# One modulation chunk per k tile, the first of them multiplied ahead of x and its sums, with idle products before it

## The chip, the cores and the metric

The kernel runs on one core of one Trainium2 chip. The metric is device time in microseconds (us) of one execution, as the median of several runs; less is better. The engines are TensorE (PE, its weight loads PEld), VectorE (DVE), ScalarE (ACT), GpSimd (POOL) and SyncE (SP), which issues most of the DMAs.

## What is computed

One step of a diffusion backbone with one trunk layer, for 128 context tokens and 512 latent tokens, 640 tokens in all, each 1024 wide. Cut to what the change touches:

```python
mod_ctx = jax.nn.silu(c_ctx)[None, :] @ w_mod[l] + b_mod[l]      # context tokens
mod_lat = jax.nn.silu(c) @ w_mod[l] + b_mod[l]                   # latent tokens
shift1, scale1, gate1, shift2, scale2, gate2 = [m[:, None, :] for m in jnp.split(mod, 6, axis=-1)]
h = _rmsnorm(x, g_norm1) * (1 + scale1) + shift1
proj = h @ w_in + b_in
q_raw, k_raw, v_raw, o_raw, gates, u_pool, g_a, g_b = jnp.split(proj, split_at, axis=-1)
```

Behind this come the mLSTM, the pooling branch, the merge, a mixture of 16 experts and a final norm. They are computed as before. So all 640 tokens need the sum of the squares of their 1024 elements (`_rmsnorm`), and each of the 1024 channels needs its shift1 and scale1 for two conditioning vectors, before any column of `w_in` can be multiplied.

## The kernel before

x lies with channels on partitions, in eight k tiles of 128 channels by 640 tokens (`xT[:, k, :]`). Every engine's program is written out by hand and runs strictly in that order; semaphores join them. The start of the kernel, which is the part that changes, is this:

- **SP** (lines 436 to 459) issues on one queue: all constants (`small`, 1440 columns), the four DMAs of x (two k tiles each), the gate weights `wgr`, and then the weight stream `wst`, 1 MB chunks in a fixed order, through four buffers (`raw`). Chunk 0 (`AT_U0`) is the first half of the pool columns of `w_in`; chunks 1 to 8 (`AT_M1`, `N_MOD1`) are the columns of `w_mod` for shift1 and scale1; chunk 9 (`AT_U1`) is the second half of the pool columns. A chunk is issued when its buffer is free (`raw_free`).
- **ACT** (698 to 722) applies tanh to the conditioning vectors, squares the eight k tiles into `hn`, rounds `wgr` and chunk 0 into their high parts, forms the reciprocal norm `rstd` with Ln and Exp (`inv_rms`), and then, for each of four pairs of k tiles, copies one row of modulation products out of PSUM (`mrow1`), forms `hn = hn * gain + shift` (L717, in two parts, context and latent), and copies it rounded to `hhi` (L721).
- **DVE** (1145 to 1186) finishes silu (`csil`), adds the eight squares up in `hn[:, 0]` (L1158), forms the low parts of the weights, multiplies x by `rstd` (L1165), forms `mod` and `gain` of each pair (L1179, L1182) and the low part `hlo = hn - hhi` (L1169).
- **PE** (2038 to 2056): `square_sums` multiplies the summed squares by a matrix of ones (two f32 products of 320 columns); `mod_pair(i)` takes two chunks (8 f32 products of 512 columns, four side by side in the array) and gives shift1 and scale1 of two k tiles, as rows; `mod_turned(i)` turns these rows to columns with four small products; `pool_outer(k)` adds k tile k to the gate and pool outputs, 18 products of 320 columns, each operand in a high and a low part (`three`). All of it stands in this order, with the `pool_outer` of early k tiles between the modulation products of later ones:

```python
            square_sums(hn, s_sum1, s_norm)
            pe.wait_ge(s_csil, 3)
            mod_pair(0)
            mod_turned(0)
            mod_pair(1)
            pe.wait_ge(s_gw, 2)
            pe.wait_ge(s_norm, 2)
            chunk_split(0)
            pool_outer(0)
            mod_turned(1)
            pool_outer(1)
            mod_pair(2)
```

After the eighth `pool_outer` the second half of the pool columns follows, and then the rest of the kernel, a PE stream with few gaps.

An f32 product leaves two records in the trace, so eight records of line 1964 are four products, or one chunk. Products whose operands are rounded (`hhi`, `hlo`, `whi` and the like) leave one. `keep_busy(n)` (1941) issues n f32 products of 256 columns on constants whose result nobody reads; the kernel uses it around the router.

Of the kernel before, what the change touches and what calls it, by code (L numbers as in the profile page):

```python
# [54 lines left out]
N_MOD1 = 8  # L55
N_U, N_GE, N_Q, N_K, N_MOD2, N_V, N_O, N_GL, N_B, N_A, N_OUT = 2, 6, 4, 4, 16, 4, 4, 2, 2, 4, 4
# [13 lines left out]
C_ID, C_ONE, C_FWD, C_BWD, C_STRICT, C_IOTA, C_NEGF, C_NEGB = (P * i for i in range(8))  # L70
C_MF = 8 * P
# [14 lines left out]
S_COL = 1088  # L86
# [39 lines left out]

def split_no(c):
    if c > AT_V:
        return N_U + N_K + 1 + c - AT_V
    if c >= AT_K:  # L130
        return N_U + 1 + (c - AT_K + 2) // 5
    return 1 if c == AT_U0 else 2
# [28 lines left out]
def raw_slot(c):  # L161
    return (c - AT_O) % 2 if AT_O <= c < AT_A else c % NRAW
# [22 lines left out]
def layer_kernel(nc, x_d, small_d, wst_d, wg_d, wpool_d, st_d, rcnt_d,  # L185
                 wexp_d, xt_d, gf_d, bv_d, y_d, so_d, mo_d):
    ctx = ExitStack()
    with ctx:
# [45 lines left out]
        rstd = at("rstd", 172.5, [P, T])  # L234
        QK = at("QK", 112, [P, 2 * H, T])
# [4 lines left out]
        mrow1 = at("mrow1", TMP + 5, [P, 2, 512])  # L240
# [127 lines left out]
        def f32(t):  # L368
# [15 lines left out]
        s_csil, s_sq, s_norm, s_hn, s_hhi, s_hlo = (sem(n) for n in (  # L384
            "s_csil", "s_sq", "s_norm", "s_hn", "s_hhi", "s_hlo"))
        d_wg, s_gain = sem("d_wg"), sem("s_gain")
# [50 lines left out]
        def _(sp):  # L437
            sp.dma_start(small[:, :], small_d).then_inc(d_const, 16)
            for k in range(0, KT, 2):
                sp.dma_start(xT[:, k:k + 2, :], x_d[:, k:k + 2, :]).then_inc(d_tile[k // 2], 16)  # L440
            sp.dma_start(wgr[:, :, :], wg_d).then_inc(d_wg, 16)
# [8 lines left out]
            for c in range(N_DENSE):  # L450
# [4 lines left out]
                sp.dma_start(raw[s][:, :], wst_d[c, :, :]).then_inc(raw_full[s], 16)  # L455
                if c == AT_V + 1:
# [57 lines left out]
        def _(gp):  # L514
# [58 lines left out]
            gp.wait_ge(s_modT, 6)  # L573
# [107 lines left out]
        def _(act):  # L681
# [21 lines left out]
            act.wait_ge(d_wg, 16)  # L703
            act.activation(wgh[:, :, :], wgr[:, :, :], ACT.Copy).then_inc(s_gw, 1)
            act.preload_act_table_set(LN_EXP)
            split_hi(0, QH[0])
            act.wait_ge(s_norm, 1)
            inv_rms(halves(rstd[:, :]), ps[:, 0:2, 0:HALF], D, s_norm)
            for i in range(4):
                chunk_used(act, AT_M1 + 2 * i + 1)  # L710
                if i >= 2:
                    act.wait_ge(s_modT, i - 1)
                act.activation(mrow1[:, i % 2, :], ps[:, 4, :], ACT.Copy).then_inc(s_mrow, 1)
                act.wait_ge(s_gain, i + 1)
                for k in (2 * i, 2 * i + 1):
                    for c, a, b in ((0, 0, TC), (1, TC, T)):
                        act.activation(hn[:, k, a:b], hn[:, k, a:b], ACT.Identity,  # L717
                                       bias=mod[:, k, c:c + 1], scale=gain[:, k, c:c + 1])\
                           .then_inc(s_hn, 1)
                    act.wait_ge(s_hn, 2 * k + 2)  # L720
                    act.activation(hhi[:, k, :], hn[:, k, :], ACT.Copy).then_inc(s_hhi, 1)  # L721
# [78 lines left out]
            def mod_row2(i):  # L800
                chunk_used(act, m2_chunk(KT * i + KT - 1))
                if i:
                    act.wait_ge(s_modT, i + 4)
# [197 lines left out]
            act.preload_act_table_set(LN_EXP)  # L1001
            act.activation(strict[:, :], cst[:, C_STRICT:C_STRICT + P], ACT.Copy)
# [128 lines left out]
        def _(dve):  # L1131
# [21 lines left out]
            st.on(dve.tensor_scalar(half_gn[:, :], col[:, G_N:G_N + KT], 0.5, None, ALU.mult))  # L1153
            for k in range(1, KT):
# [7 lines left out]
            split_lo(0, QH[0], QL[0])  # L1162

            def normalise(k):
                st.on(dve.tensor_tensor(hn[:, k, :], xT[:, k, :], rstd[:, :], ALU.mult))  # L1165

            def input_lo(k):
                dve.wait_ge(s_hhi, k + 1)
                dve.tensor_tensor(hlo[:, k, :], hn[:, k, :], f32(hhi[:, k, :]), ALU.subtract)\  # L1169
                   .then_inc(s_hlo, 1)  # L1170

            dve.wait_ge(s_norm, 2)
            for k in range(4):
                normalise(k)
            for i in range(4):
                dve.wait_ge(s_modT, i + 1)
                both = mod[:, 0:16, :].rearrange("p (s k) c -> p s k c", s=2)[:, :, 2 * i:2 * i + 2, :]
                bias = col[:, B_MOD:B_MOD + 16].rearrange("p (s k) -> p s k", s=2)
                st.do(dve.tensor_tensor(both, ps[:, 5, 0:8].rearrange(  # L1179
                    "p (s k c) -> p s k c", s=2, c=2), by(bias[:, :, 2 * i:2 * i + 2].unsqueeze(3),  # L1180
                                                          [P, 2, 2, 2]), ALU.add))
                dve.scalar_tensor_tensor(  # L1182
                    gain[:, 2 * i:2 * i + 2, :], mod[:, 8 + 2 * i:10 + 2 * i, :], 1.0,
                    by(col[:, G_1 + 2 * i:G_1 + 2 * i + 2].unsqueeze(2), [P, 2, 2]), ALU.add, ALU.mult)\
                   .then_inc(s_gain, 1)
                if i < 2:
                    normalise(4 + 2 * i)
                    normalise(5 + 2 * i)
                for k in (2 * i, 2 * i + 1):
                    input_lo(k)  # L1190
# [116 lines left out]
            def mod_add(i):  # L1307
                dve.wait_ge(s_modT, i + 5)
# [174 lines left out]
            dve.wait_ge(s_gt, 3)  # L1483
            mask_maxima(0)
# [432 lines left out]
        def _(pe):  # L1917
# [41 lines left out]
            def mod_half(c, kh, bank):  # L1959

                slot = raw_slot(c)
                pe.wait_ge(raw_full[slot], (raw_use(c) + 1) * 16)
                for kk in range(4):
                    last = nc.tensor.matmul(  # L1964
                        ps[32 * kk:32 * kk + 32, bank, :], csil[:, 4 * kh + kk, :],
                        raw[slot][:, kk * 512:(kk + 1) * 512], start=kh == 0, stop=kh == 1,
                        tile_position=(0, 32 * kk))
                last.then_inc(raw_free[slot], 1)
# [11 lines left out]
            def mod_columns(rows, out):  # L1980
                for b in range(4):
                    last = mm(out[:, 2 * b:2 * b + 2], rows[:, b * P:(b + 1) * P],
# [11 lines left out]
            def pool_outer(k):  # L1994
                pe.wait_ge(s_hlo, k + 1)
                last = three([(ps[0:GP, 6 + a, 0:HALF], cut_half(a)) for a in range(2)],
                             wgh[:, k, :], wgl[:, k, :], hhi[:, k, :], hlo[:, k, :],
                             k == 0, k == KT - 1)
                if k == KT - 1:
                    last.then_inc(s_gate, 1)  # L2000
                for b in range(2):
                    o = (b * KT + k) * P
                    last = three([(ps[:, 2 * b + a, 0:HALF], cut_half(a)) for a in range(2)],
                                 QH[0][:, o:o + P], QL[0][:, o:o + P], hhi[:, k, :], hlo[:, k, :],
                                 k == 0, k == KT - 1)
# [657 lines left out]
```

## Time and profile before

| | |
|---|---|
| median of 3 runs | 968.03 us (966.66 to 969.24) |
| profiled execution, its own time | 965.73 us |
| its span | 963.9 us |
| PE busy | 929.9 us, 96% of the span |
| DVE, ACT, POOL busy | 698.6, 495.3, 134.8 us |
| moved by DMA | 229.51 MB, mean 238 GB/s |

The span is the time from the first to the last instruction in the trace; 1.8 us of the execution lie around it. PE is busy in nearly all of the span except its first fortieth, where its digit in the page's slices is 3.

### The profile page before, as it was taken

To read this page: it belongs to the slowest core of one execution; us is meant where nothing else is said; L and a number is where in the kernel's file an instruction comes from. 1 tells how busy PE (TensorE), PEld (TensorE's weight loads), DVE (VectorE), ACT (ScalarE), POOL (GpSimd) and SP (SyncE) were. 2 spreads that over 40 slices of the span, in tenths; PEclk is the share of its full clock that TensorE was granted. 3 is DMA by queue.
4 is the path that set the end of the run, shared out by engine and by line. 5 is a ranking of instruction groups with operands and counts; after the bars stand their busy time and mean duration, and the time that the engine had idled before them with its cause. 6 is when DMAs were issued, how large, how long until landed. Compare 5 with 4: busy or idle time off the path is not lost.

```text
span 963.9 us, 14007 instructions
## 1 busy us (share of the span) xinstructions
PE 929.9 (96%) x5518; PEld 819.8 (85%) x5518; DVE 698.6 (72%) x895; ACT 495.3 (51%) x656; POOL 134.8 (14%) x141
## 2 busy tenths in 40 slices
PE   3999999999999999999999999989999999999986
PEld 1799999988788999999999988868888888888862
DVE  5398777649223478889454546369999999999998
ACT  5565442231222356666411232246788787887863
POOL 0000000089920111000000000020111111111100
PEclk9999999999999999999999999979999999999998
DMA  9812443287762342434382155159999999999964
GB/s 380 335 45 90 152 134 101 83 333 274 278 258 113 91 135 87 122 121 161 136 338 88 44 188 227 45 197 394 421 421 404 422 416 411 420 414 419 392 274 163
DMA packets 39201, 229.51 MB, mean 238 GB/s; under 512 B 4288, under 2 KB 4480, under 8 KB 18528
## 3 DMA queue, kind: packets, MB, share of 16 engines
q1 hardware_dynamic: 26496, 180.25, 47.6%
q0 software_dynamic: 10048, 41.70, 12.2%
q10 hardware_dynamic: 2592, 6.66, 1.8%
q8 instruction: 44, 0.72, 0.3%
q14 instruction: 21, 0.17, 0.0%
HBM read 205.94 MB, written 22.66 MB: 237 GB/s over the span
## 4 chain that ended last, share of the span: by engine, by line
PE 92%; DMA 4%; DVE 3%; ACT 1%; issue 0%; SPq 0%; DVEq 0%; POOLq 0%; ACTq 0%
PE ps L1919 86%; PE ps L2444 2%; PE ps L1975 2%; DMA h2scr<-ht 1%; DMA xT<-in_x 1%; PE ps L2472 1%; DMA raw<-in_wst 1%; PE ps L1964 1%; DMA xg<-h2scr,slot_rows 0%; PE ps L2286 0%; PE ps L2187 0%; DVE rowA L1874 0%; DVE xr L1877 0%; DVE xr L1881 0%; PE ps L2363 0%
## 5 line engine op out<-in xcount | busy, mean ns | idle before, releaser
L690 ACT ACTIVATE whi<-raw 128x2048 fp32r<-128x2048 f32 x19 | 36.3, 1912 | 96.6 <-PE ps L1919 63.7
L1919 PE MATMUL ps<-hhi,whi 128*128 128x320 f32 x352 | 81.2, 312 | 0.0
L1919 PE MATMUL ps<-hlo,whi 128*128 128x320 f32 x352 | 80.2, 309 | 0.0
L1919 PE MATMUL ps<-hhi,wlo 128*128 128x320 f32 x352 | 80.2, 309 | 0.0
L1730 DVE TENSOR_TENSOR olo<-raw,ohi 128x2048 fp32r<-128x2048 f32 x32 | 72.3, 2286 | 3.9 <-ACT ohi L1042 3.9
L1138 DVE TENSOR_TENSOR wlo<-raw,whi 128x2048 fp32r<-128x2048 f32 x19 | 43.9, 2311 | 42.0 <-ACT whi L690 42.0
L1730 DVE TENSOR_TENSOR wlo<-raw,whi 128x2048 fp32r<-128x2048 f32 x31 | 70.3, 2288 | 5.3 <-ACT whi L1042 4.7
L1042 ACT ACTIVATE whi<-raw 128x2048 fp32r<-128x2048 f32 x32 | 61.3, 1918 | 18.4 <-PE ps L1919 18.4
L1042 ACT ACTIVATE ohi<-raw 128x2048 fp32r<-128x2048 f32 x32 | 61.3, 1917 | 18.0 <-PE ps L1919 18.0
L1919 PEld LDWEIGHTS ps<-hhi,whi 128*128 128x128 f32 x352 | 58.6, 188 | 6.2 <-issue 5.0
L1919 PEld LDWEIGHTS ps<-hhi,wlo 128*128 128x128 f32 x352 | 58.9, 188 | 0.0
L1919 PEld LDWEIGHTS ps<-hlo,whi 128*128 128x128 f32 x352 | 58.8, 188 | 0.0
L1919 PE MATMUL ps<-whi,xgh 128*128 128x512 f32 x128 | 50.9, 398 | 0.0
L1919 PE MATMUL ps<-ohi,xgh 128*128 128x512 f32 x128 | 50.8, 397 | 0.0
L1919 PE MATMUL ps<-ohi,xgl 128*128 128x512 f32 x128 | 50.0, 391 | 0.0
L1919 PE MATMUL ps<-whi,xgl 128*128 128x512 f32 x128 | 50.0, 390 | 0.0
L1919 PE MATMUL ps<-wlo,xgh 128*128 128x512 f32 x128 | 49.8, 389 | 0.0
L1919 PE MATMUL ps<-olo,xgh 128*128 128x512 f32 x128 | 49.8, 389 | 0.0
L1919 PE MATMUL ps<-Tlo,ghi 128*128 128x320 f32 x160 | 49.4, 309 | 0.0
L1919 PE MATMUL ps<-Thi,ghi 128*128 128x320 f32 x160 | 49.4, 309 | 0.0
L1919 PE MATMUL ps<-hhi,owh 128*128 128x320 f32 x160 | 49.3, 324 | 0.1
L1919 PE MATMUL ps<-hhi,owl 128*128 128x320 f32 x160 | 46.9, 309 | 0.0
(424 smaller groups left out, 2551.3 us busy)
## 6 DMA issues: line engine op xcount, KB each, us to landing
raw<-in_wexp SPq DMA_DIRECT2D x64, 1024.0 KB, 9.0
raw<-in_wst SPq DMA_DIRECT2D x60, 1024.0 KB, 6.1
eraw<-in_wexp SPq DMA_DIRECT2D x32, 1024.0 KB, 8.8
nm<-negscr POOLq DMA_DIRECT2D x8, 640.0 KB, 7.1
wib<-wiscr POOLq DMA_DIRECT2D x8, 512.0 KB, 6.3
thscr<-gout ACTq DMA_DIRECT2D x12, 320.0 KB, 5.2
TH<-thscr POOLq DMA_DIRECT2D x3, 1280.0 KB, 7.4
xT<-in_x SPq DMA_DIRECT2D x4, 640.0 KB, 7.1
```

What stands on the lines that cost most here:

```text
L690: act.activation(dst[:, :], raw[raw_slot(c)][:, :], ACT.Copy).then_inc(hi_ready, 1)
L1042: act.activation(ehi[i % ESPL][:, :], eraw[s][:, :], ACT.Copy).then_inc(e_hi, 1)
L1138: dve.tensor_tensor(lo[:, :], raw[s][:, :], f32(hi[:, :]), ALU.subtract)\
L1730: dve.tensor_tensor(elo[i % ESPL][:, :], eraw[s][:, :], f32(ehi[i % ESPL][:, :]), ALU.subtract).then_inc(e_free[s], 1)
L1919: return nc.tensor.matmul(out, lhsT, rhs, start=start, stop=stop)
L1964: last = nc.tensor.matmul(ps[32 * kk:32 * kk + 32, bank, :], csil[:, 4 * kh + kk, :], raw[slot][:, kk * 512:(kk + 1) * 512], start=kh == 0 ...
L1975: last = nc.tensor.matmul(ps[32 * g:32 * g + 32, 6, :], csil[:, k, :], raw[slot][:, g * 512:(g + 1) * 512], start=k == 0, stop=k == KT - 1 ...
L2444: last = nc.tensor.transpose(ps[:, 6 + k // 4, (k % 4) * P:(k % 4 + 1) * P], xg[b][:, k * P:(k + 1) * P], ident)
L2472: last = nc.tensor.transpose(ps[:, 2 * (p % 2), f * P:(f + 1) * P], act_[:, f * P:(f + 1) * P], ident)
```

## The change

It has four parts, all in the start of the kernel.

1. **The modulation goes by k tile.** The eight chunks of `w_mod` are laid out anew on the host, so that one chunk holds shift1 and scale1 of one k tile (256 columns, all 1024 inputs) instead of half the inputs of two k tiles. `mod_product(k)` has 8 products of 256 columns and `mod_turned(k)` two small ones. `outer_hi(k)` and `outer_lo(k)` are the 18 products of `pool_outer(k)`, in two parts.
2. **The first chunk comes ahead.** SP issues a part of the constants (360 columns), then modulation chunk 0, and only then x. PE multiplies it ahead of `square_sums`, and DVE's `mod_row(0)` and `gains(0)` stand ahead of the sums of squares.
3. **Idle products.** Before `mod_product(0)` PE runs 28 f32 products of 186 columns on constants, whose result nobody reads.
4. **Parted loads and other edges.** Chunk 0 of the weights has a buffer of its own (`u0r`) and comes in two DMAs, rounded in three parts; the rest of the constants comes after the last modulation chunk (`d_late`). ACT writes `hhi` straight from x in one step, and DVE forms the unrounded `hn` itself (`modulated`). The constants' columns are in another order.

```diff
-            sp.dma_start(small[:, :], small_d).then_inc(d_const, 16)
-            for k in range(0, KT, 2):
-                sp.dma_start(xT[:, k:k + 2, :], x_d[:, k:k + 2, :]).then_inc(d_tile[k // 2], 16)
-            sp.dma_start(wgr[:, :, :], wg_d).then_inc(d_wg, 16)
+            sp.dma_start(small[:, C_ONE:S_WR], small_d[:, C_ONE:S_WR]).then_inc(d_const, 16)
...
+                if c == AT_M1:
+                    for k in range(0, KT, 2):
+                        sp.dma_start(xT[:, k:k + 2, :], x_d[:, k:k + 2, :]).then_inc(d_tile[k // 2], 16)
+                    sp.dma_start(wgr[:, :, :], wg_d).then_inc(d_wg, 16)
+                    sp.dma_start(u0r[:, U0_PART[0]], wst_d[AT_U0, :, U0_PART[0]]).then_inc(d_wg, 16)
...
             def input_hi(k):
+                act.wait_ge(*((s_gain, k + 1) if k else (s_norm, 3)))
+                for c, a, b in ((0, 0, TC), (1, TC, T)):
+                    act.activation(hhi[:, k, a:b], xT[:, k, a:b], ACT.Identity,
+                                   bias=mod[:, k, c:c + 1], scale=gain[:, k, c:c + 1]).then_inc(s_hhi, 1)
...
+            def mod_row(k):
+                chunk_used(dve, AT_M1 + k)
+                dve.tensor_copy(mrow1[:, k % 4, :], ps[:, 4, 0:2 * P]).then_inc(s_mrow, 1)
...
+            mod_row(0)
+            gains(0)
             for k in range(1, KT):
                 dve.wait_ge(s_sq, k + 1)
...
+            normalise(0)
+            st.wait()
+            dve.sem_inc(s_norm, 1)
+            modulated(0)
+            mod_row(1)
+            normalise(1)
+            input_lo(0)
...
             pe.wait_ge(d_const, 16)
+            for _ in range(28):
+                mm(ps[:, 3, 0:C_END - C_ONE], ones, cst[:, C_ONE:C_END], True, True)
+            pe.wait_ge(s_csil, 3)
+            mod_product(0)
+            mod_turned(0)
             square_sums(hn, s_sum1, s_norm)
-            pe.wait_ge(s_csil, 3)
-            mod_pair(0)
-            mod_turned(0)
-            mod_pair(1)
...
+            mod_product(1)
+            mod_turned(1)
+            mod_product(2)
             pe.wait_ge(s_norm, 2)
...
+            for k in range(KT):
+                outer_hi(k)
+                if k + 2 < KT:
+                    mod_turned(k + 2)
+                outer_lo(k)
+                if k + 3 < KT:
+                    mod_product(k + 3)
```

On PE, from the program's start to the first product of k tile 0 (`small` are constants, among them the ones, `csil` the conditioning, `raw` a modulation chunk, `hn` the squares, `mrow` the modulation as rows), before:

```order
L1919 MATMUL ps<-hn,small 128x320 [waits s_sum1,d_const]
L1919 MATMUL ps<-hn,small 128x320
L1964 MATMUL ps<-raw_69,csil 32x512 [waits raw_full1,s_csil]
L1964 MATMUL ps<-raw_69,csil 32x512 x3
L1964 MATMUL ps<-raw_70,csil 32x512 [waits raw_full2]
L1964 MATMUL ps<-raw_70,csil 32x512 x3
L1919 MATMUL ps<-small,mrow_85 128x2 [waits s_mrow]
L1919 MATMUL ps<-small,mrow_85 128x2 x3
L1964 MATMUL ps<-raw_71,csil 32x512 [waits raw_full3,s_mrow]
```

and the same place in the changed kernel:

```order
L1978 MATMUL ps<-small 128x186 [waits d_const]
L1978 MATMUL ps<-small 128x186 x27
L2025 MATMUL ps<-raw_69,csil 32x256 [waits raw_full1,s_csil]
L2025 MATMUL ps<-raw_69,csil 32x256 x7
L1978 MATMUL ps<-small,mrow_86 128x2 [waits s_mrow]
L1978 MATMUL ps<-small,mrow_86 128x2
L1978 MATMUL ps<-hn,small 128x320 [waits s_sum1]
L1978 MATMUL ps<-hn,small 128x320
L2025 MATMUL ps<-raw_70,csil 32x256 [waits raw_full2,s_mrow]
L2025 MATMUL ps<-raw_70,csil 32x256 x7
L1978 MATMUL ps<-small,mrow_86 128x2 [waits s_mrow,s_gain]
```

The idle products stand first now, then the first modulation chunk and its turning, and the sum of squares moved from the first place behind them.

On DVE, from the end of silu to the first normalised tile, before:

```order
L1153 TENSOR_SCALAR half_gn<-small 128x8
L1158 TENSOR_TENSOR hn<-hn 128x640 [waits s_sq]
L1158 TENSOR_TENSOR hn<-hn 128x640 [waits s_sum1,s_sq] x6
L1160 TENSOR_TENSOR wgl<-wgr,wgh 128x384 [waits s_gw]
L1138 TENSOR_TENSOR wlo_74<-raw_68,whi_72 128x2048 [waits hi_ready]
L1165 TENSOR_TENSOR hn<-xT,rstd 128x640 [waits s_norm]
```

and in the changed kernel:

```order
L1183 TENSOR_SCALAR half_gn<-small 128x8
L1186 COPY mrow_86<-ps 128x256 [waits raw_free1]
L1191 TENSOR_TENSOR mod<-ps,small 128x2x2 [waits s_modT]
L1194 SCALAR_TENSOR_TENSOR gain<-mod,small 128x2 [waits dve_steps]
L1204 TENSOR_TENSOR hn<-hn 128x640 [waits s_sq]
L1204 TENSOR_TENSOR hn<-hn 128x640 [waits s_sum1,s_sq] x6
L1206 TENSOR_TENSOR wgl<-wgr,wgh 128x384 [waits s_gw]
L1212 TENSOR_TENSOR wlo_74<-u0r,whi_72 128x512 [waits hi_ready]
L1216 TENSOR_TENSOR xT<-xT,rstd 128x640 [waits s_norm]
L1221 TENSOR_SCALAR hn<-xT,gain,mod 128x128 [waits dve_steps,s_gain]
L1221 TENSOR_SCALAR hn<-xT,gain,mod 128x512
L1186 COPY mrow_86<-ps 128x256 [waits raw_free2]
```

Three instructions moved ahead of the sums of squares: the copy of the first modulation row, which waits until PE has used the chunk (`raw_free1`), and the two that form gain 0.

## Rows read from the trace of the kernel before

**Rows 1.** The page, part 4: the chain that ended last, by engine.

```profile
PE 92%; DMA 4%; DVE 3%; ACT 1%; issue 0%; SPq 0%; DVEq 0%; POOLq 0%; ACTq 0%
```

**Rows 2.** Timeline, first 13 us: start, length (us), engine, line, operation, [idle before].

```profile
0.75 0.39 SPq L438 DMA_DIRECT2D small<-in_small  x1
...
4.85 0.22 ACT L698 ACTIVATE csil<-small 128x16 f32<-128x16 f32 x1 [2.49 <-DMA small<-in_small]
...
6.58 1.36 ACT L702 ACTIVATE hn<-xT 128x640 f32<-128x640 f32 x2 [1.51 <-DMA xT<-in_x]
7.97 0.82 DVE L1158 TENSOR_TENSOR hn<-hn 128x640 f32<-128x640 f32 x1 [2.18 <-ACT hn L702]
...
11.40 1.36 ACT L702 ACTIVATE hn<-xT 128x640 f32<-128x640 f32 x2 [0.26 <-DMA xT<-in_x]
```

**Rows 3.** Timeline: sums of squares, first modulation chunks, norm.

```profile
14.58 2.47 PE L1919 MATMUL ps<-hn,small 128*128 128x320 f32 x4 [14.58 <-DVE hn L1158]
...
16.98 1.94 PE L1964 MATMUL ps<-raw,csil 128*32 128x512 f32 x8
17.09 0.79 ACT L694 ACTIVATE rstd<-ps,small 128x640 f32<-128x640 f32 x1 [0.69 <-PE ps L1919]
...
18.68 3.03 DVE L1165 TENSOR_TENSOR hn<-xT,rstd 128x640 f32<-128x640 f32 x4
...
19.33 1.06 PE L1964 MATMUL ps<-raw,csil 128*32 128x512 f32 x8 [0.41 <-DMA raw<-in_wst]
20.46 0.60 ACT L713 ACTIVATE mrow<-ps 128x512 f32<-128x512 f32 x1 [1.81 <-PE ps L1964]
...
21.11 1.05 PE L1919 MATMUL ps<-small,mrow 128*128 128x2 f32 x8 [0.72 <-ACT mrow L713]
...
22.20 0.17 DVE L1179 TENSOR_TENSOR mod<-ps,small 128x8 f32<-128x8 f32 x1 [0.49 <-PE ps L1919]
...
22.60 1.20 ACT L717 ACTIVATE hn<-hn,mod,gain 128x128 f32<-128x128 f32 x2 [1.54 <-DVE gain L1182]
```

**Rows 4.** The chain in order of time, merged: start, length, what.

```profile
26.00 6.21 PE ps L1919 x44
32.21 1.85 PE ps L1964 x16
...
48.99 51.10 PE ps L1919 x347
```

**Rows 5.** Stretches: length, busy (x instructions) of PE, PEld, DVE, ACT, POOL, PE clock, DMA share, GB/s.

```profile
14.50:16.00 1.50, 1.42 (x3) 1.06 (x4) 0.40 (x1) 1.50 (x1) 0.00 (x0) 1.00 1.02 426
...
22.00:23.00 1.00, 1.00 (x10) 0.23 (x9) 0.76 (x3) 0.40 (x1) 0.00 (x0) 0.62 1.03 426
...
25.00:26.00 1.00, 1.00 (x9) 0.07 (x2) 0.43 (x1) 0.97 (x2) 0.00 (x0) 0.68 0.99 410
```

**Rows 6.** Timeline of PE at `keep_busy`, and the clock in the stretches beside it.

```profile
631.92 4.61 PE L1919 MATMUL ps<-small 128*128 128x256 f32 x10
636.33 0.29 PE L1919 MATMUL ps<-am,strict 128*128 128x96 bf16 x1
...
635.00:636.00 1.00, 1.00 (x4) 0.77 (x3) 0.86 (x7) 1.00 (x2) 0.00 (x0) 0.50 0.98 410
636.00:637.00 1.00, 1.00 (x10) 0.70 (x9) 0.75 (x5) 1.00 (x1) 0.00 (x0) 0.68 1.04 434
```

**Rows 7.** Timeline: the first k tile, the wait at the seventh, the second pool half.

```profile
25.93 0.49 PE L1919 MATMUL ps<-hhi,wgh 128*48 128x320 f32 x2
...
48.99 0.49 PE L1919 MATMUL ps<-hhi,wgh 128*48 128x320 f32 x2 [0.65 <-DVE hlo L1169]
...
51.77 2.29 DVE L1138 TENSOR_TENSOR wlo<-raw,whi 128x2048 fp32r<-128x2048 f32 x1 [0.97 <-ACT whi L690]
```

**Rows 8.** Groups of DVE instructions by form: busy, mean ns of one.

```profile
L1647 DVE COPY lt<-ps 128x128 f32<-128x128 f32 x1 | 0.3, 290 | 2.1 <-PE ps L2414 2.1
```

More of the change, by code:

```diff
@@ L67 @@
 N_DENSE = AT_OUT + N_OUT
-C_ID, C_ONE, C_FWD, C_BWD, C_STRICT, C_IOTA, C_NEGF, C_NEGB = (P * i for i in range(8))
-C_MF = 8 * P
+C_ID, C_STRICT, C_IOTA, C_NEGF, C_NEGB, C_ONE = (P * i for i in range(6))
+C_MF = 6 * P
 C_MB = C_MF + 1
@@ L448, in _ @@
                 sp.sem_inc(d_gb[t], 16)
-            for c in range(N_DENSE):
+            for c in range(AT_M1, N_DENSE):
                 s = raw_slot(c)
@@ L455, in _ @@
                 sp.dma_start(raw[s][:, :], wst_d[c, :, :]).then_inc(raw_full[s], 16)
+                if c == AT_M1:
[3 more added lines that the diff above has]
+                    sp.dma_start(u0r[:, U0_PART[0]], wst_d[AT_U0, :, U0_PART[0]]).then_inc(d_wg, 16)
+                if c == AT_M1 + 2:
+                    rest = slice(U0_PART[1].start, CH)
+                    sp.dma_start(u0r[:, rest], wst_d[AT_U0, :, rest]).then_inc(d_u0, 16)
+                if c == AT_M1 + N_MOD1 - 1:
+                    for part in (slice(0, C_ONE), slice(S_WR, S_END)):
+                        sp.dma_start(small[:, part], small_d[:, part]).then_inc(d_late, 16)
                 if c == AT_V + 1:
@@ L1167, in input_lo, with modulated @@
+            def modulated(k):
+                dve.wait_ge(s_gain, k + 1)
+                for c, a, b in ((0, 0, TC), (1, TC, T)):
+                    st.on(dve.tensor_scalar(hn[:, k, a:b], xT[:, k, a:b], gain[:, k, c:c + 1],
+                                            mod[:, k, c:c + 1], ALU.mult, ALU.add))
             def input_lo(k):
-                dve.wait_ge(s_hhi, k + 1)
+                dve.wait_ge(s_hhi, 2 * k + 2)
+                st.wait()
                 dve.tensor_tensor(hlo[:, k, :], hn[:, k, :], f32(hhi[:, k, :]), ALU.subtract)\
@@ L1170, in input_lo @@
                    .then_inc(s_hlo, 1)
+            u0_lo(0)
             dve.wait_ge(s_norm, 2)
[L1173 to L1190, printed above, removed]
+            normalise(0)
@@ L1191, in _ @@
+            st.wait()
+            dve.sem_inc(s_norm, 1)
[3 more added lines that the diff above has]
+            input_lo(0)
+            for k in range(1, KT):
+                gains(k)
+                modulated(k)
+                if k == 2:
+                    u0_lo(1)
+                if k < KT - 1:
+                    normalise(k + 1)
+                input_lo(k)
+                if k == 2:
+                    u0_lo(2)
             split_lo(AT_U1, QH[1], QL[1])
@@ L1483, in _ @@
             dve.wait_ge(s_gt, 3)
+            dve.wait_ge(d_late, 32)
             mask_maxima(0)
@@ L1978, in mod2_product, with mod_turned @@
                 last.then_inc(raw_free[slot], 1)
-            def mod_columns(rows, out):
-                for b in range(4):
-                    last = mm(out[:, 2 * b:2 * b + 2], rows[:, b * P:(b + 1) * P],
+            def mod_turned(k):
+                if k:
+                    pe.wait_ge(s_gain, k)
+                pe.wait_ge(s_mrow, k + 1)
+                for b in range(2):
+                    last = mm(ps[:, 5, 2 * b:2 * b + 2], mrow1[:, k % 4, b * P:(b + 1) * P],
                               cst[:, C_CMB:C_CMB + 2], True, True)
@@ L1991, in square_sums @@
                 last.then_inc(done, 1)
-            def pool_outer(k):
-                pe.wait_ge(s_hlo, k + 1)
[L1996 to L2005, printed above, removed]
-                    if k == KT - 1:
-                        last.then_inc(u_ready, 1)
@@ new lines, in outer_hi, with outer_lo @@
+            def outer_hi(k):
+                pe.wait_ge(s_hhi, 2 * k + 2)
+                if k in (0, 2, 4):
+                    pe.wait_ge(s_gw, 3 + k // 2)
+                for groups, hi, lo, _ in outer_groups(k):
+                    for out, part in groups:
+                        mm(out, hi, part(hhi[:, k, :]), k == 0, False)
+                    for out, part in groups:
+                        mm(out, lo, part(hhi[:, k, :]), False, False)
+            def outer_lo(k):
+                pe.wait_ge(s_hlo, k + 1)
+                for groups, hi, _, done in outer_groups(k):
+                    for out, part in groups:
+                        last = mm(out, hi, part(hlo[:, k, :]), False, k == KT - 1)
+                    if k == KT - 1:
+                        last.then_inc(done, 1)
```

143 lines of the change are left out of this document (78 added, 65 removed).

## The prediction

> **What bounds the kernel now.** I read the page's chain first: TensorE (PE) holds 92% of it [rows 1]. The chain in order of time then shows that from 25.93 us on PE runs nearly without a gap: two `pool_outer` and a turning in 6.21, a modulation pair in 1.85, and so on, with one stall of about 0.8 us ahead of 48.99, then 51.10 in a piece [rows 4, 7]. All the time this edit can touch is therefore when the product stream of k tile 0 starts (25.93 now) and how much work or waiting lies between that start and the end of the eighth tile; what comes later is the same stream and moves as a whole. Before 25.93 the timeline shows a chain over all engines: x lands and ACT squares it (last two squares at 11.40, 1.36), DVE adds, PE multiplies the sum by ones at 14.58, ACT forms Ln and Exp from 17.09, DVE normalises from 18.68 [rows 2, 3].
>
> **The clock.** The same eight records of a chunk take 1.94 at 16.98 and 1.06 at 19.33 [rows 3]: PE was at its lower level (1.2 GHz) and had risen to 2.4 GHz in between, 4.3 to 4.8 us after its first product at 14.58. The clock column shows 1.00 there [rows 5]; it only follows from the first recorded change on, so I go by the pace of the records. Later the column does follow: 0.62 in 22 to 23 means full until 22.24 and half after it, 0.68 in 25 to 26 means back at 25.64, so 3.4 us at half after a stretch with gaps in PE's work [rows 3, 5]. At `keep_busy` it was at half from before 631.92 until 636.64, 4.7 us into those products [rows 6].
>
> **Part 3, the idle products, is the term that decides.** `keep_busy` has the same kind of product: 10 records of 256 columns from 631.92 to the next instruction at 636.33 are 0.441 each at the lower clock [rows 6]. 28 products of 186 columns are 56 records; by columns 0.32 each at half, 0.16 at full. They start when the first constants land. Those were 720 KB and in at 4.83; x came at 3 x 640 KB in 4.82 (6.58 to 11.40), 0.41 MB per us, so 180 KB land 1.35 earlier, at 3.5 [rows 2]. Slow for the first 3.4 to 4.8 us, taken as 4.1 (13 records), then 43 at 0.16: 6.8. They end at 3.5 + 10.9 = 14.4. Bounds: 12.3 if all are fast (8.8), 21.4 if none is (17.9); the rise is seen in every such place, so I stay at 14.4. Modulation chunk 0, which they stand before, lands at about 6.2: constants and chunk are 1.23 MB against the 1.39 MB that are in at 6.56 now [rows 2].
>
> On record length the Trainium skill ("TensorE: Matmul & The Clock Gate", Back-to-back issue gap) gives columns over 1.2 GHz for a matmul at the low clock, which for 28 matmuls of 186 columns would be an estimate of 4.3 us and an end at 7.9. The rows disagree by four for these f32 products, two records each of twice that length: 0.441 us a record of 256 columns.
>
> **Part 2, the order on DVE.** The sums of squares now stand behind `mod_row(0)` and `gains(0)`, and these wait for `mod_product(0)`, hence for the idle products. Step by step: the chunk's product is 16 records of 256 columns, as many columns as the eight of 512: 19.33 to 20.46 at full clock, 1.13, to 15.6 [rows 3]. DVE's copy of 256 columns lies between the 0.29 of a 128-column copy and the 0.60 of ACT's 512 columns: 0.4, to 16.0 [rows 3, 8]. Turning has half the records of 1.05: 0.6 with the handover, to 16.6; `mod` and `gain` 22.20 to 22.60, 0.4, to 17.0 [rows 3]. Now the seven adds, 0.82 each, each waiting for the one before, 0.85: 5.95, to 22.95 [rows 2]. Without those three instructions ahead they would have ended with x: it lands with 1 MB more before it and 0.55 MB less, last square at about 14.0, last add at 14.9. So the wait placed on DVE costs eight microseconds of the norm's chain; queued behind it are all seven adds, and PE's `square_sums`, ACT's Ln and everything of x wait for them.
>
> From 16.6 to 22.95 PE has nothing: its next instruction in order is `square_sums`. The gaps ahead of 22.24 were shorter and the clock fell; I take it as fallen, so the square sums take what they took at 14.58, 2.5, to 25.45 (1.3 if not fallen), Ln and Exp 1.6, to 27.05 [rows 3]. Next DVE `normalise(0)` 0.85, to 27.9, while PE works off `mod_product(1)`, at half clock 1.94, to 27.4. DVE `modulated(0)` is two instructions with no row of before: above zero, below two adds (1.65); ACT's same shapes take 1.20 together [rows 3]; 0.85, to 28.75. `mod_row(1)` 0.4, to 29.15. Then PE, in order, `mod_turned(1)` 0.5 and `mod_product(2)` 0.95 (half of the 1.85 for a pair [rows 4]) before `outer_hi(0)`: 30.6. Its `hhi(0)` is there at 27.95 + 1.2 = 29.15, in time. The stream starts 4.7 later than at 25.93.
>
> **Part 1, the work behind the start.** Before: 28.35 us from 25.93 to the end of tile 7, at 54.3, which is 48.99 and two tiles more (two tiles and one stretch of turning in 6.21 make 2.64 a tile, eight 21.1; two pairs 3.7; three turnings 2.8; the stall 0.8) [rows 4, 7]. After: eight tiles 21.1, five products 4.65, six turnings of two 3.0, together 28.8, and no stall, since turning runs two tiles ahead of its use. That is 0.45 more: one product more is left behind the start. The second pool half needs ACT's and DVE's split of its chunk: last turning, then gain 0.4, `input_hi` 1.2, ACT 1.9, DVE 2.29, 5.9 in all, under the 6.15 (two tiles and a low part) that PE works on; now it is as tight (54.06 against 54.3) [rows 7]. If that cover were gone it would cost its own excess, 0 to 0.5.
>
> **Part 4** costs nothing: the parts of chunk 0 are in before 21 and rounded under the waits above; ACT loses a copy per tile and DVE gains two instructions, but a tile leaves DVE some 3 us (0.4, 0.85, 0.76, 0.83) under PE's 2.64 + 0.95 + 0.5. For tiles 6 and 7 this is nearly level; 0 to 0.5. The late constants are 0.4 MB, 1 us on a queue with room, and wanted long after; without room their price would be that 1 us.
>
> **Sum:** 4.7 + 0.45 = 5.1 us later. Against the profiled execution, 965.7 + 5.1 = 970.8; the median stands 2.3 above that execution, so 968.0 + 5.1 = **973.1**. Own range, with the bounds of the small terms: 971.5 to 974.5.
>
> **Rivals.**
> - **The clock is not up when tile 0 starts.** PE's second busy stretch runs 22.95 to 27.4, then 1.75 us wait for the turning; a rise came 3.4 to 4.8 us after starts from half, so it is close. If missed: turning +0.4, product +0.95, and tile 0 at half for another 1.7. About 3 more: 976.1. For it: the narrow margin; against: 4.45 us of unbroken work. Chance 0.15.
> - **The clock is up all along.** Idle products in 8.8 (end 12.3), square sums 1.3 instead of 2.5: 3.4 less, 969.7, within 0.3% of before. For it: the column's 1.00; against: the slow records under that same 1.00 [rows 3, 5]. Chance 0.12.
> - **The idle products are short**: one record each at a cycle a column, 0.155 at half clock, 4.3 in all. They would end at 7.9 and the adds at 16.4; start of tile 0 at 24.1, with the 0.45 a gain of 1.4: 966.6. Against: every f32 row has two records of twice that. Chance 0.04. This is the case that the Trainium skill's gap would give.
> - **Faster: the first chunk is wholly hidden under x.** If the idle products end with its landing at 6.2, `gains(0)` is over at 9 and the adds end with x at 14.9; tile 0 starts at 22.5 and the change gains about 3: 965.1. This side decides from an end of the idle products below about 9.3 (gain zero; 6.4 for a gain of 0.3%). Against: 56 records do not fit, even fast. Chance 0.04.
> - **The change does not do what it says later on:** a wait on transfers absorbs the delay. PE holds the chain [rows 1], so there is little of this: 969. Chance 0.05.
>
> **How the numbers follow.** The likeliest case has 0.60. 0.3% is 2.9 us, about what a measurement of this kernel can tell from no change. Faster by more than that: 0.05, the fourth rival and a bit. Within: 0.18 (clock up, short products with part of their chance, absorption). Slower: 0.77 (likeliest and the missed rise, with a little of their overlap). The range for 8 in 10 reaches from the clock-up case, 969.3, to the missed rise with its terms, 976.8.
>
> **What would show it.** Right: in the changed kernel's timeline 56 records on constants of 0.32 and then 0.16 us, ending near 14.4; a DVE wait for PE up to 15.6; seven adds in a row from 17 to 23; a PE gap of 6 us before slow square sums; tile 0 near 30.6 and the eighth tile's end near 59.4. Wrong: idle products gone before 9, adds that follow the squares tile by tile, or tile 0 before 26.

## The result, and the profile after

The change makes the kernel slower. Its median is 973.63 us (972.27 to 977.59, 11 runs) beside 968.00 us (966.26 to 970.79, 11 runs) of the kernel before on the same chips: a ratio of 1.0062, 95% interval 1.0049 to 1.0074, or 5.6 us by the medians. The forecast was 973.1 us, in a range from 969.3 to 976.8. The profiled execution after took 972.83 us with a span of 971.0, 7.1 us more than the profiled one before; of these 7.1, the walk below finds 7.5 in the first 62 us and -0.4 in all the rest.

The chain of waits of the changed kernel in order of time (start, length in us, what), from the first constants to the second tile:

```profile
0.75 2.38 DMA small<-in_small
...
3.17 11.21 PE ps L1978 x56
14.39 1.05 PE ps L2025 x16
...
15.46 0.44 DVE mrow L1186
...
15.94 0.62 PE ps L1978 x4
...
16.58 0.18 DVE mod L1191
...
17.78 0.84 DVE hn L1204
...
23.31 2.52 PE ps L1978 x4
25.85 0.80 ACT rstd L709
...
27.44 0.84 DVE xT L1216
...
29.70 0.58 PE ps L1978 x4
30.27 1.00 PE ps L2025 x16
31.27 4.69 PE ps L1978 x22
...
36.97 3.15 PE ps L1978 x22
```

In the kernel before, this chain ran over x and its squares, but from there not over the norm. The chain of before in order of time goes on with ACT's rounding of the first pool chunk, DVE's low part of it, and the transfer of the fourth modulation chunk, which needs the buffer that this step frees:

```profile
14.49 1.92 ACT whi L690
...
16.43 2.30 DVE wlo L1138
...
18.75 5.49 DMA raw<-in_wst
...
24.29 1.71 PE ps L1964 x8
```

So tile 0 of the kernel before waited for that chunk, and the norm, which the prediction named in its account of the start, had some time to spare. In the changed kernel the chain runs over 56 records of idle products, which end at 14.39, the first chunk's product, DVE's copy of its row, the turning, gain 0, and only then the seven adds (L1204, 16.94 to 23.27). The arrival of x no longer appears in it. The timeline shows the same from DVE's side, with the wait and who ended it in brackets:

```profile
13.55 1.36 ACT L717 ACTIVATE hn<-xT 128x640 f32<-128x640 f32 x2 [0.22 <-DMA xT<-in_x]
...
15.46 0.42 DVE L1186 COPY mrow<-ps 128x256 f32<-128x256 f32 x1 [11.36 <-PE ps L2025]
16.86 6.39 DVE L1204 TENSOR_TENSOR hn<-hn 128x640 f32<-128x640 f32 x7
23.31 2.50 PE L1978 MATMUL ps<-hn,small 128*128 128x320 f32 x4 [6.76 <-DVE hn L1204]
```

DVE sits 11.36 us before the copy, and PE 6.76 us before the square sums, which take 2.50, about as at 14.58 in [rows 3] (2.47). All squares were there at 14.9.

The clock, by stretches of the changed kernel (length; busy of PE, PEld, DVE, ACT, POOL; granted clock; DMA share; GB/s):

```profile
9.00:14.00 5.00, 5.00 (x34) 5.00 (x33) 0.00 (x0) 4.34 (x7) 0.00 (x0) 1.00 1.00 393
...
17.00:20.00 3.00, 0.00 (x0) 0.00 (x0) 2.69 (x4) 0.27 (x1) 0.00 (x0) 0.63 0.99 419
20.00:22.00 2.00, 0.00 (x0) 0.00 (x0) 1.79 (x3) 0.00 (x0) 0.00 (x0) 0.50 1.04 437
...
28.00:29.00 1.00, 0.00 (x0) 0.00 (x0) 0.86 (x3) 0.64 (x2) 0.00 (x0) 0.99 0.49 66
...
31.00:32.00 1.00, 1.00 (x12) 0.63 (x5) 0.93 (x5) 0.66 (x2) 0.00 (x0) 0.71 0.82 344
32.00:33.00 1.00, 1.00 (x6) 1.00 (x5) 1.00 (x2) 1.00 (x3) 0.00 (x0) 0.50 0.95 172
```

The idle products bring PE to 2.4 GHz (34 records in the 5 us from 9 to 14, 0.15 each), and in the gap behind the turning it falls to 1.2 GHz within 17 to 20. It is back at about 28.0 and falls again at about 31.4, 0.2 us into tile 0, behind a gap of PE of 2.02 us. Tile 0 and what stands in it take 4.69 in place of the 3.15 of tile 1: 1.5 us for this second fall. The kernel before has a fall at 22.24 too, but it ends at 25.64, before tile 0 [rows 5].

Tile 0 starts at 31.20 (25.93 before, [rows 7]); the second pool half, and with it the stream that is alike in both kernels, starts at 61.83, against 54.31 before (48.99 and two tiles, [rows 7]).

### The profile page after: what moved, and what is told of

The parts are those of the page before. It is cut to its first block, busy times and chain, and to the rows that moved or that the text cites. A ratio compares the mean times of both kernels' runs of the same rounds, so it can differ in the third digit from the quotient of the medians.

```text
span 971.0 us, 14294 instructions
## 1 busy us (share of the span) xinstructions
PE 940.1 (97%) x5638; PEld 833.6 (86%) x5638; DVE 707.5 (73%) x923; ACT 490.2 (50%) x652; POOL 138.6 (14%) x141
## 4 chain that ended last, share of the span: by engine, by line
PE 92%; DVE 4%; DMA 2%; issue 1%; ACT 1%; DVEq 0%; POOLq 0%; ACTq 0%
PE ps L1978 86%; PE ps L2036 2%; PE ps L2505 1%; DMA h2scr<-ht 1%; PE ps L2025 1%; PE ps L2533 1%; DVE hn L1204 1%; DMA xg<-h2scr,slot_rows 1%; PE ps L2347 0%; PE ps L2248 0%; DMA yscr<-yb,slot_rows 0%; DVE rowA L1933 0%; DVE xr L1936 0%; DVE xr L1940 0%; PE ps L2424 0%
## 5 line engine op out<-in xcount | busy, mean ns | idle before, releaser
L1789 DVE TENSOR_TENSOR wlo<-raw,whi 128x2048 fp32r<-128x2048 f32 x31 | 70.3, 2289 | 4.6 <-ACT whi L1072 4.6
L1168 DVE TENSOR_TENSOR wlo<-raw,whi 128x2048 fp32r<-128x2048 f32 x18 | 41.9, 2329 | 39.4 <-ACT whi L705 39.4
L662 POOL DMA_INDIRECT yscr<-yb,slot_rows x16 | 27.0, 1687 | 145.8 <-ACT yb L1092 133.2
```

The source lines that it names most:

```text
L662: gp.indirect_dma_start(yscr, bass.IndirectOffsetOnAxis(ap=slot_rows[:, 1, e:e + 1], axis=0), yb[p % 2][:, :], None).then_inc(d_sc, 16)
L1168: dve.tensor_tensor(lo[:, :], raw[s][:, :], f32(hi[:, :]), ALU.subtract)\
L1789: dve.tensor_tensor(elo[i % ESPL][:, :], eraw[s][:, :], f32(ehi[i % ESPL][:, :]), ALU.subtract).then_inc(e_free[s], 1)
```

## The experiments

Two theories went into all of them. **A:** the loss is a wait handed on: DVE's copy of the first modulation row stands ahead of the sums of squares, PE reaches the product it copies only behind the idle products, and so their end sets the norm; the falls of the clock come on top. **B**, in several forms: the loss lies in the new order by k tile, in the clock alone, or in having the chunk ahead of x at all. Each kernel was timed beside the kernel before in the same session; ratios are to that. The start of the second pool half, read from each kernel's timeline, places the profiled execution: 54.3 before, 61.8 in the changed kernel.

| kernel | median, us | ratio to before, 95% interval | second pool half starts |
|---|---|---|---|
| changed | 973.63 | 1.0062 (1.0049 to 1.0074) | 61.83 |
| idle36 | 977.09 | 1.0081 (1.0059 to 1.0102) | 66.87 |
| idle8 | 968.66 | 1.0001 (0.9989 to 1.0014) | 55.51 |
| sums_first | 967.17 | 0.9994 (0.9981 to 1.0008) | 53.85 |
| before_idle22 | 968.58 | 1.0010 (0.9996 to 1.0023) | 57.23 |
| row1_early | 963.20 | 0.9951 (0.9938 to 0.9963) | 51.39 |
| row1_no_idle | 966.78 | 0.9989 (0.9979 to 0.9999) | 53.15 |
| held_clock | 972.06 | 1.0040 (1.0028 to 1.0052) | 59.69 |
| idle_behind | 966.54 | 0.9985 (0.9971 to 0.9999) | 54.92 |
| row1_alone | 972.36 | 1.0047 (1.0031 to 1.0064) | 59.70 |
| row1_idle16 | 965.63 | 0.9980 (0.9968 to 0.9991) | 55.81 |

### More and fewer idle products

`idle36` and `idle8` change one number.

```diff
-            for _ in range(28):
+            for _ in range(36):
```

> The changed kernel with 36 idle products in place of 28, nothing else. Theory A (the idle products end late and DVE's row copy, standing ahead of the sums of squares, hands their end on to the whole norm chain): they end 8 x 2 records x 0.16 us = 2.55 us later at the full clock, near 16.95, and everything behind moves by that: 2.5 slower than the changed kernel, about 976.2. Theory B (the loss is in the new order by k tile and its turnings and waits, or in the second fall of the clock at 31.4, and the idle products only fill time that PE waits anyway): no change against the changed kernel, 973.6, within 0.5.

Measured: 977.09 us, 3.5 over the changed kernel by the medians, 1.9 by the ratios (1.0081 against 1.0062); the expected 2.55 lies between. The intervals of the two ratios overlap, so the times alone do not rule out B's "no change"; the trace does. The chain of `idle36` shows the handing on, link by link:

```profile
3.27 14.64 PE ps L1978 x72
17.90 1.04 PE ps L2025 x16
...
26.82 2.51 PE ps L1978 x4
```

In this execution the idle products end 3.5 later than in the changed kernel's (17.90 against 14.39), 0.9 more than eight products at full clock would add, since the slow pace lasted longer at the start; and the square sums start 3.5 later (26.82 against 23.31). The second pool half starts 5.0 later, because more of the work ahead of and in tile 0 ran at half clock (the third chunk's product took 1.86 in place of 1.00).

> The changed kernel with 8 idle products in place of 28. Theory A: 16 records at 0.32 end at 8.3 in place of 14.4; the adds start near 11 and end near 17.4, the product stream of tile 0 starts near 25.3 in place of 31.2; 5 to 6 faster than the changed kernel if the clock behaves alike, so 967 to 969, about level with before. Theory B: the loss stays, 973 or more, since a PE that did less stands at the lower clock longer.

Measured: 968.66 us, level with before and inside the expected range. The timeline of `idle8` agrees with the walk: product at 8.04, seven adds from 10.58, and from its chain the square sums at 17.04:

```profile
3.19 4.93 PE L1978 MATMUL ps<-small 128*128 128x186 f32 x16 [3.19 <-DMA small<-in_small]
8.04 1.07 PE L2025 MATMUL ps<-raw,csil 128*32 128x256 f32 x16
...
10.58 6.40 DVE L1204 TENSOR_TENSOR hn<-hn 128x640 f32<-128x640 f32 x7
```

Twenty idle products fewer give 5.0 us back. That, with the chain of `idle36`, shows the length of the idle products to be on the path of the changed kernel.

### All idle products, but nothing waits for them

```diff
-            mod_row(0)
-            gains(0)
             for k in range(1, KT):
                 dve.wait_ge(s_sq, k + 1)
...
+            mod_row(0)
             dve.wait_ge(s_gw, 1)
...
             u0_lo(0)
+            gains(0)
             dve.wait_ge(s_norm, 2)
...
             mod_product(0)
-            mod_turned(0)
             square_sums(hn, s_sum1, s_norm)
+            mod_turned(0)
             mod_product(1)
```

> The changed kernel with all 28 idle products, but on DVE the copy of the first modulation row stands behind the seven adds and gain 0 behind the low part of the first pool chunk, and on PE the square sums stand ahead of the first turning. Theory A: the adds follow the squares tile by tile and end near 15.8, the square sums run at the full clock and end near 17.1, DVE normalises near 18.7, tile 0 starts near 22.5 (31.2 in the changed kernel); its end lies 3 us before that of the kernel before, or 1.3 if the clock falls in the gap ahead of tile 0: 965 to 966.7. Theory B: the loss stays for the larger part, 971 or more.

Measured: 967.17 us, within the noise of before and 6.5 below the changed kernel, with the same 28 idle products; that is 0.5 above the expected range. From the chain of `sums_first`, the adds now follow x, and the square sums run at the full clock:

```profile
3.00 7.17 DMA xT<-in_x
...
15.61 0.84 DVE hn L1202
16.49 1.36 PE ps L1978 x4
17.88 0.80 ACT rstd L709
...
22.30 1.71 PE ps L2025 x16
24.01 4.00 PE ps L1978 x22
```

The norm comes 0.8 later than worked out (DVE normalises at 19.47, 18.7 expected): the adds start at 10.00, as soon as two tiles are squared, but take 0.93 each from start to start, more than the 0.8 in which ACT squares a tile, and so end at 16.45 in place of 15.8. The stretch behind the norm was expected too short as well: tile 0 starts at 23.94, not 22.5. Two terms are in that: the clock fell in the gap ahead (stretches 22 to 24 and 24 to 26 of `sums_first` below; tile 0 takes 4.00), and PE waits 2.54 for DVE's copy of the second row.

```profile
21.16 0.42 DVE L1186 COPY mrow<-ps 128x256 f32<-128x256 f32 x1
...
21.72 0.58 PE L1978 MATMUL ps<-small,mrow 128*128 128x2 f32 x4 [2.54 <-DVE mrow L1186]
```

```profile
22.00:24.00 2.00, 2.00 (x20) 0.87 (x20) 1.82 (x6) 0.00 (x0) 0.00 (x0) 0.61 0.99 410
24.00:26.00 2.00, 2.00 (x10) 1.79 (x9) 1.53 (x3) 1.94 (x5) 0.00 (x0) 0.53 1.03 434
```

### What a warm PE is worth in the kernel before

```diff
             pe.wait_ge(d_const, 16)
+            for _ in range(22):
+                mm(ps[:, 3, 0:186], ones, cst[:, 0:186], True, True)
             square_sums(hn, s_sum1, s_norm)
```

> The kernel before with 22 idle products ahead of the square sums, ending near 14, when the summed squares are ready at 14.6. It shows what a clock that is up is worth by itself. Theory A: little, since the square sums end 1.2 earlier but DVE still works on the first pool chunk's low part until 18.7 and the modulation chunks arrive no earlier; 0 to 1 faster, 967 to 968. Theory B (the low clock at the start is itself worth 2 us or more): 966 or less.

Measured: 968.58 us, ratio 1.0010, no gain that can be told from none, and 0.6 above A's range; B's 966 or less is out. The square sums did get shorter, but DVE normalises at the same time, 18.70 against 18.68 in [rows 3], since it is still on the low part of chunk 0:

```profile
14.62 1.30 PE L1919 MATMUL ps<-hn,small 128*128 128x320 f32 x4
16.36 0.78 ACT L694 ACTIVATE rstd<-ps,small 128x640 f32<-128x640 f32 x1
16.49 2.29 DVE L1138 TENSOR_TENSOR wlo<-raw,whi 128x2048 fp32r<-128x2048 f32 x1 [1.50 <-ACT whi L690]
...
18.70 3.02 DVE L1165 TENSOR_TENSOR hn<-xT,rstd 128x640 f32<-128x640 f32 x4
...
25.33 1.94 PE L1964 MATMUL ps<-raw,csil 128*32 128x512 f32 x8 [2.06 <-DMA raw<-in_wst]
```

The fourth modulation chunk, for which tile 0 waits in this kernel, lands in this execution 1.0 later than in that of before (its product starts at 25.33, not 24.29). PE is at half clock again by then (1.94 us) and stays so into tile 0, which puts its second pool half at 57.23; its span, 966.7, is 2.8 over the profiled one of before. So this kernel shows that faster square sums buy nothing in the kernel before, but not what a clock that stays up would be worth there.

### The second row's copy ahead of the norm

`row1_early` is `sums_first` with one more DVE instruction moved:

```diff
             gains(0)
+            mod_row(1)
             dve.wait_ge(s_norm, 2)
...
             modulated(0)
-            mod_row(1)
             normalise(1)
```

> sums_first with one more step moved: DVE copies the second modulation row ahead of its wait for the norm in place of behind the first modulated tile. Theory A (what still holds tile 0 back is PE's wait for that copy, 2.5 us, in which the clock falls again): PE does the second turning and the third product under Ln and Exp, tile 0 starts when its high part is there, near 21.7 in place of 23.9, and without a stretch at half clock; 3 faster than sums_first, 963.5 to 964.5, faster than before by 0.4%. Theory B (tile 0 is held by the norm alone and the clock falls anyway): 966 to 967, as sums_first.

Measured: 963.20 us (962.55 to 964.17, 5 runs), ratio 0.9951, interval 0.9938 to 0.9963. This version, 0.3 below the expected range, beats both kernels, before by 0.5% and the changed one by 10.4 us. In its timeline the copy stands at the end of ACT's Exp, the turning and the third product run while ACT and DVE prepare tile 0, and tile 0 starts at 21.91, 4.0 earlier than in the kernel before; and the clock stays up.

```profile
19.37 0.42 DVE L1186 COPY mrow<-ps 128x256 f32<-128x256 f32 x1 [0.67 <-PE ps L2025]
...
19.94 0.58 PE L1978 MATMUL ps<-small,mrow 128*128 128x2 f32 x4 [0.64 <-DVE mrow L1186]
...
21.91 0.46 PE L1978 MATMUL ps<-hhi,wgh 128*48 128x320 f32 x2 [0.38 <-issue]
```

```profile
22.00:24.00 2.00, 2.00 (x16) 1.93 (x16) 1.82 (x6) 0.65 (x3) 0.00 (x0) 1.00 1.03 434
24.00:26.00 2.00, 2.00 (x24) 1.22 (x23) 1.87 (x4) 2.00 (x3) 0.00 (x0) 1.00 1.00 418
```

That it can start earlier than before fits what the chain of before shows: the first pool chunk now has a buffer of its own, and three modulation chunks stand ahead of tile 0 in place of four. No kernel here changes that alone, so this part is not shown.

The next kernel, `row1_alone`, makes the same move in the changed kernel and leaves the rest:

```diff
             u0_lo(0)
+            mod_row(1)
             dve.wait_ge(s_norm, 2)
...
             modulated(0)
-            mod_row(1)
             normalise(1)
```

> The changed kernel with only DVE's copy of the second modulation row moved ahead of its wait for the norm. The idle products still hand their end on to the adds. Theory A (two separate losses: the adds' wait, and PE's wait of 2 us for this copy with the fall of the clock behind it): square sums at half clock as in the changed kernel, the second chunk's product ends near 27.7, its copy then holds the norm by 0.7, but turning and third product are done by 30 and tile 0 starts near 30 in place of 31.2 without a later fall: 2 to 3 faster than the changed kernel, 970.5 to 971.5, still slower than before. Theory B (row1_early was fast because of the copy alone): 965 or less.

Measured: 972.36 us, 1.3 below the changed kernel where 2 to 3 was expected; the intervals of the two ratios overlap (1.0031 to 1.0064 against 1.0049 to 1.0074), so by the times alone a gain is not shown. In the profiled execution tile 0 starts at 30.22, as expected, without a later fall, and the second pool half 2.1 earlier. B is out: the copy alone does not make the fast version; the adds' wait is by far the larger part.

### The clock held up in the changed kernel

```diff
             mod_turned(0)
+            idle(19)
             square_sums(hn, s_sum1, s_norm)
             mod_product(1)
+            pe.wait_ge(s_norm, 2)
+            idle(5)
             mod_turned(1)
```

(`idle(n)` issues n of the 28 products' kind.)

> The changed kernel with its order and its 28 idle products, and 19 more between the first turning and the square sums and 5 more behind the norm, to fill the gaps of PE. It shows how much of the loss is the clock's alone. Theory A: square sums 1.3 in place of 2.5 (1.2 gained), no half clock in tile 0 (1.7 gained), the adds' wait unchanged: 2 to 3 faster than the changed kernel, 970.5 to 971.5, and its runs closer together. Theory B (the loss is the clock's altogether): level with before, 968.

Measured: 972.06 us (970.98 to 973.48), 1.6 below the changed kernel, less than the 2 to 3 expected; the intervals of the two ratios just overlap. Its runs lie closer together, as expected. The clock was held, as its chain shows: square sums in 1.36, tile 0 in 3.14.

```profile
23.88 1.36 PE ps L1978 x4
...
30.68 3.14 PE ps L1978 x22
```

The second pool half starts at 59.69, 2.1 earlier, although in this execution the first 28 idle products ended 0.6 later (14.96). So the clock has about 1.6 of the 5.6 us by the medians, and in the profiled executions 2.1, or 2.7 without that late end, of 7.5. Some 4 remain with the clock up (ratio 1.0040, interval above 1): form B "it is all the clock" is out. (The filled products ahead of the square sums ended at 23.2 and held nobody.)

### The chunk ahead of x, undelayed

```diff
-            for _ in range(28):
-                mm(ps[:, 3, 0:C_END - C_ONE], ones, cst[:, C_ONE:C_END], True, True)
+            idle(4)
             pe.wait_ge(s_csil, 3)
             mod_product(0)
             mod_turned(0)
+            idle(16)
             square_sums(hn, s_sum1, s_norm)
```

> The changed kernel with its DVE order, but only 4 idle products ahead of the first modulation product, and 16 behind its turning, ahead of the square sums. Theory A (that chunk may well go ahead of x if nothing delays it): the product starts near 6.3 when its chunk lands, gain 0 is there near 10, the adds start then and end near 17, the square sums run at the full clock, tile 0 starts near 24; about as sums_first, 966.5 to 968. Theory B (a row copy ahead of the sums is itself the loss): 972 or more.

Measured: 966.54 us. DVE's order is the changed kernel's, with copy and gain 0 ahead of the sums, and yet the loss of 5.6 is gone. The chunk lands and is multiplied at 7.36 (at half clock), and the adds start at 11.16:

```profile
7.36 1.94 PE L2025 MATMUL ps<-raw,csil 128*32 128x256 f32 x16 [1.32 <-DMA raw<-in_wst]
...
10.71 6.92 PE L1978 MATMUL ps<-small 128*128 128x186 f32 x32
...
11.16 6.39 DVE L1204 TENSOR_TENSOR hn<-hn 128x640 f32<-128x640 f32 x7
...
17.61 1.34 PE L1978 MATMUL ps<-hn,small 128*128 128x320 f32 x4
```

A row copy ahead of the sums thus costs little in itself (the adds end at 17.5, against 16.45 in `sums_first`); it does harm behind 28 idle products. The 16 idle products end together with the adds, and the square sums behind them run at the full clock. Tile 0 starts at 24.35, again at half clock.

### What the idle products are worth once nothing waits for them

`row1_no_idle` and `row1_idle16` are `row1_early` with 0 and 16 idle products (the edit of the second):

```diff
-            for _ in range(28):
+            for _ in range(16):
```

> row1_early without any idle product. It shows what the idle products are worth once nothing waits for their end. Theory A: the square sums take 2.5 in place of 1.3, the second chunk 1.9 in place of 1.1, and the copy of its row now holds DVE ahead of the norm; tile 0 starts 2.5 to 3 later than in row1_early, 966 to 967.5. Theory B (idle products are worth nothing here): within 0.5 of row1_early.

> row1_early with 16 idle products in place of 28, which then end near 9.5; PE has 1.1 us of product behind them and then 6 us of nothing before the square sums. Theory A (what the idle products must do is reach up to the square sums, and not merely raise the clock once): square sums and second chunk at half clock as in row1_no_idle, 966 to 967.5. Theory B (the rise once is enough): as row1_early, 963 to 964.

Measured: 966.78 and 965.63 us. Against `row1_early` (963.20) the idle products are worth 3.6 us; 16 of them, which end at 11.0 with 4.6 us of nothing between the first chunk's product and the square sums, give 1.1 us of that, and by the ratios (0.9980 and 0.9989, intervals that overlap) even this is not clear of nothing. In both the square sums run at half clock, 2.50 us in `row1_no_idle`. So it matters that they reach up to the square sums, and A's expectation holds, though `row1_idle16` lies 0.4 below its range. `idle_behind` supports it: its 20 products, 16 of them right ahead of the square sums, give these the full clock (1.34 us), which 16 early ones do not. The time of these two differs from one execution to the next (963.89 to 968.82 without idle products; 962.55 to 964.17 in `row1_early`): in the profiled one of `row1_no_idle` the clock was up from tile 0 on, in that of `row1_idle16` it was at half until past 28, and the latter's pool half starts later, though its median is lower.

## Why the prediction was right, point by point

| step | predicted | in the changed kernel's trace |
|---|---|---|
| first constants in | 3.5 | 3.13 |
| 56 idle records | 10.9, to 14.4 | 11.2, to 14.39 |
| first chunk's product, to 15.6 | 1.13 | 1.05, to 15.44 |
| DVE's copy of 256 columns | 0.4 | 0.44 |
| gain 0 done | 17.0 | 16.94 |
| seven adds, to 22.95 | 5.95 | 6.33, to 23.27 |
| square sums at half clock | 2.5 | 2.52 |
| DVE normalises | 27.05 | 27.44 |
| tile 0 starts | 30.6 | 31.20 |
| from tile 0 to the end of tile 7 | 28.8 | 30.63 |
| later than before, sum | 5.1 | 7.5 in this execution; 5.6 by the medians |

**Which path decides** was right, and three kernels show it: `idle8` and `idle_behind` shorten what DVE's copy waits for, `sums_first` takes the adds out from behind it, and each gives the loss back. The delay also reached the end undiminished but for 0.4 us, so the rival of a wait that absorbs it is out.

**The account of the kernel before** was wrong at one place: it put the norm on the chain ahead of 25.93, where the trace has the fourth modulation chunk (the chain lines in the section on the result). The sum took the 25.93 as measured and did not suffer by it; but it is why `before_idle22` gains nothing.

**The adds** were a little short: 0.93 from start to start, 0.84 of work and 0.09 of handover, not 0.85. The statement that without the three instructions they would have ended with x, at 14.9, making the wait cost eight microseconds, does not hold: `sums_first` ends them at 16.45, so the wait cost 6.8. The rows of before showed it already, for there the square sums start 1.8 behind the end of the last square at 12.76 [rows 2, 3]. The sum does not use this figure; the gain of 3 in the rival "faster" does.

**The work behind the start** was the term mis-sized: 0.45 forecast, 2.25 in the profiled execution (30.63 against 28.38 before). 1.5 of it is the second fall of the clock in tile 0. That is part of the rival "the clock is not up when tile 0 starts", in another form than it was told: the rise was not missed, it came at 28.0, in the gap where it was weighed, and was lost again at 31.4. The likeliest case took the clock as staying up from there. The rest, some 0.3, is five products at 1.00 each in place of 0.93. The stall before 48.99 is gone, as forecast; and the second pool half does not wait for its split.

**The other rivals.** "Up all along" is out; the slow records were the truth and the column's 1.00 was not. "Short" products are out too: 56 records took 11.21 us, not 4.3. "Faster" needed idle products that end below 9.3: `idle8` ends its own at 8.1 and stands level, with a fall of the clock in tile 0 that the rival had not priced; `row1_no_idle` has none and is faster by 0.1%, at the edge of its interval. The price of transfers was set a little low: chunk 0 landed near 7.3, not 6.2, and the last square ended at 14.9, not 14.0, because SP issued the chunk at 2.15, and x behind it. It was off the path.

**What helped by luck.** The terms were read from one execution of before (965.73) that lies below all 11 timed ones, and the median moved less (5.6) than the profiled executions did (7.1). The term of 1.5 that was missed in the profile is therefore barely seen in the median, and that the median came within 0.5 of the forecast is in part luck: by the trace the sum was 2.4 too small. Of the 11 runs of the changed kernel four lie between 976.4 and 977.6, the others between 972.3 and 974.7. The mean granted clock on record is 0.977 to 0.981 in these four and 0.981 to 0.985 in the others. That fits executions in which the clock stands lower for longer, as that rival forecast (976.1), but none of the four was profiled, so where it stood lower stays open.

## What to carry to other kernels

Products that only keep TensorE busy are work in its queue like any other: price them by records of their own kind (f32 here: two records each, 0.32 us for 186 columns at the low clock), end them before the first thing that somebody waits for, and let them reach up to the next real product, or they buy little. When a step is moved ahead on one engine, look at what its wait holds back there: an instruction that waits for TensorE ahead of seven adds put everything of x behind TensorE's idle products, and with the same step behind the adds the loss was gone. And the copy that lets TensorE go on belonged ahead of the wait for the norm, not behind it: this one instruction made the difference between level with before and 0.5% faster.

## What the runs showed of the hardware

- The granted clock rose at 28.0 in the changed kernel and fell at 31.4, 0.2 us into a dense stream, behind a PE gap of 2.0 us and two short groups of products. `sums_first`, with a gap of 2.54 ahead of the same products, has the fall too; `row1_early`, with a gap of 1.34 ahead of its square sums and at most 0.64 from there to tile 0, has not, nor has `held_clock`, with gaps of at most 0.67. It stood at half until 34.84. The length of the gap alone does not settle it: in the kernel before the clock fell at 22.24, though no gap of PE since its first product was over 0.72 us [rows 3, 5].
- From PE's first product at 3.2 the slow pace lasted unequally long: 56 records took 11.21 in the changed kernel, 11.14 in `row1_alone` and 11.78 in `held_clock`; 72 took 14.64 in `idle36`, where eight products at full clock would have added 2.55 and 3.4 came; 32 took 7.92 in `row1_idle16`, where 6.4 had been expected. A design that counts on a fixed number of products to end at a given time was off by half a microsecond to one and a half here.
- The clock column reads 1.00 before the first recorded change, even where records are slow: `idle_behind` has 1.94 us for the first chunk's product at 7.36, and 1.07 for the same 16 records at 18.88.
